# Recurrence: x and z on all four blocks of the array, the identity added in the copy of prod

## The reference, cut to what matters

```
def wkv7_step(S, inp):
    r, w, k, v, a, b = inp
    sa = jnp.einsum('bhvk,bhk->bhv', S, a)
    S = S * w[:, :, None, :] + sa[..., None] * b[:, :, None, :] + v[..., None] * k[:, :, None, :]
    return S, jnp.einsum('bhvk,bhk->bhv', S, r)

for d in range(2):
    S_c, yc_d = direction(cx, d, S0)
    _, yl_d = direction(lat, d, S_c)
```

## Time and profile before

| | us |
|---|---|
| median of 3 runs | 4211.17 (4208.52 to 4217.72) |
| the profiled execution | 4217.04 |
| its span, first to last instruction | 4215.2 |
| mean granted clock of TensorE | 0.940 |

### The profile page before, as it was taken

How to read it: one execution, slowest core, us unless ns; L and a number is a source line. 1 busy time by engine, 2 the same in 40 slices (tenths; PEclk the granted TensorE clock), 3 DMA queues, 4 the chain that set the end, 5 groups by cost and what they waited for, 6 DMA issues and landing times. The chain is left out here.

```text
span 4215.2 us, 70162 instructions
## 1 busy us (share of the span) xinstructions
PE 3678.9 (87%) x29588; PEld 2620.8 (62%) x29588; DVE 2002.5 (48%) x3720; ACT 1101.5 (26%) x2219; POOL 640.1 (15%) x675
## 2 busy tenths in 40 slices
PE   5978869999979897989868777698999997899999
PEld 4844663444458774868753222297778776677877
DVE  3688750000045566757660000155567446656762
ACT  2124510000024313223220000124532223663221
POOL 0014400111113202415200000013200001440000
PEclk8988989999989998989979999999999998899999
DMA  4142258999940321010249999820122231012222
GB/s 169 61 158 61 76 212 329 393 391 391 377 148 36 98 100 53 3 42 3 69 181 394 402 405 403 336 81 21 47 95 95 93 98 42 21 35 73 94 95 80
DMA packets 195487, 659.98 MB, mean 157 GB/s; under 512 B 27708, under 2 KB 86076, under 8 KB 145368
## 3 DMA queue, kind: packets, MB, share of 16 engines
q1 hardware_dynamic: 182392, 621.16, 38.8%
q0 software_dynamic: 12784, 34.35, 3.1%
HBM read 626.01 MB, written 29.44 MB: 155 GB/s over the span
## 5 line engine op out<-in xcount | busy, mean ns | idle before, releaser
L3469 DVE TENSOR_TENSOR ffn_w_lo<-ffn_landing,ffn_w_hi 128x1024 fp32r<-128x1024 f32 x128 | 156.8, 1225 | 295.4 <-ACT ffn_w_hi L3447 295.4
L3418 PE MATMUL ffn_ps<-ffn_inT_hi,ffn_w_hi 128*128 128x512 f32 x704 | 277.8, 395 | 3.5 <-PEq L70 3.5
L3418 PE MATMUL ffn_ps<-ffn_inT_lo,ffn_w_hi 128*128 128x512 f32 x704 | 278.8, 396 | 0.0
L3418 PE MATMUL ffn_ps<-ffn_inT_hi,ffn_w_lo 128*128 128x512 f32 x704 | 277.9, 395 | 0.0
L2044 PE MATMUL up_ps<-w_quarter,rowsT 128*64 128x512 f32 x1024 | 235.9, 602 | 36.7 <-DMA w_quarter<-in_moe_w 36.7
L2044 PE MATMUL down_ps<-w_quarter,hiddenT 128*64 128x512 f32 x1024 | 235.0, 598 | 31.7 <-DMA w_quarter<-in_moe_w 29.7
L2044 PE MATMUL gate_ps<-w_quarter,rowsT 128*64 128x512 f32 x1024 | 235.5, 605 | 29.5 <-DMA w_quarter<-in_moe_w 20.7
L1960 POOL DMA_INDIRECT summed_dram<-gains_then_rows,part_row x48 | 74.7, 1556 | 929.2 <-DVE gains_then_rows L2174 924.3
L2167 DVE TENSOR_TENSOR gain_then_hidden<-up_ps,gain_then_hidden 128x768 f32<-128x768 f32 (+1 forms) x32 | 26.4, 824 | 348.3 <-PE up_ps L2056 179.0
L2044 PEld LDWEIGHTS down_ps<-w_quarter,hiddenT 128*64 128x64 f32 x1024 | 68.5, 136 | 189.3 <-issue 130.1
L2104 ACT ACTIVATE rowsT<-misc_ps 128x384 f32<-128x384 f32 (+1 forms) x64 | 27.8, 437 | 599.0 <-PE misc_ps L2033 597.3
(11 more groups left out here) (722 smaller groups left out, 8416.8 us busy)
## 6 DMA issues: line engine op xcount, KB each, us to landing
w_quarter<-in_moe_w SPq DMA_DIRECT2D x384, 1024.0 KB, 17.8
ffn_landing<-in_f_w_up SPq DMA_DIRECT2D x88, 512.0 KB, 3.5
ada_ring<-in_ada_w SPq DMA_DIRECT2D x80, 512.0 KB, 5.6
ffn_landing<-in_f_w_down SPq DMA_DIRECT2D x44, 512.0 KB, 3.5
w_landing<-in_od_w_in SPq DMA_DIRECT2D x13, 1024.0 KB, 6.3
w_landing<-in_a_w_in SPq DMA_DIRECT2D x12, 1024.0 KB, 5.1
ada_landing<-in_ada_w SPq DMA_DIRECT2D x8, 1024.0 KB, 12.6
w_landing<-in_ev_w_in SPq DMA_DIRECT2D x6, 1024.0 KB, 5.0
```

Of the source, the lines that this page charges most:

```text
L3418: mm = nc.tensor.matmul(ps[c % 4][:, :], w[:, c % NP, cols], h[:, k, :], start=(k + i == 0), stop=(k == KD - 1 and i == 2))
L3469: nc.vector.tensor_tensor(wl[:, c % NP, :], land[:, c % NL, :], wh[:, c % NP, :].bitcast(F32), ALU.subtract).then_inc(split, 1)
```

## The change

x and z are no longer increments. prod's copy adds the identity (VectorE, from PSUM, L2654 of the changed kernel), so that x_ps = (I + prod)' X and z_ps = X' (I + prod) are the new X and Z, which ScalarE copies (L2548, L2550). z is written to the other half of the partitions than x, and so is L_off's gram: prod reads half o and writes half hb, x reads hb and writes hb, z reads hb and writes o. x and z of a head are issued in turn, x, z, x, z, over four different blocks. L is kept with its halves swapped, by a gram of its own (`gram_l`, 24 matmuls into `prod_ps`), while the start of X comes from `x_ps`. At a boundary ScalarE copies the filled-in block (z_full) ahead of L. VectorE does new_state, scaled_state and output_rows after the prod adds of level 0, decay_sums and effective_keys ahead of a masked copy, and scaled_queries after the last level.

```diff
+    other = (half[1], half[0])
@@ scalar
-                for n in range(LV):
-                    rows = slice(0, P) if n < LC else co
+                for n in range(LC - 1):
                     for g in range(2):
-                        act.wait_ge(sm["prod_done"], 2 * LV * s + 2 * n + g + 1)
-                        nc.scalar.activation(Pm[g][rows, :, :], b4(bp[g])[rows], ACT.Copy).then_inc(sm["prod_kept"], 1)
+                        act.wait_ge(sm["xz_done"], 2 * LC * s + 2 * n + g + 1)
+                        nc.scalar.activation(Zb[g][:, :, :], b4(bz[g]), ACT.Copy).then_inc(sm["z_kept"], 1)
+                    for g in range(2):
+                        nc.scalar.activation(X[g][:, :, :], b4(bx[g]), ACT.Copy).then_inc(sm["x_kept"], 1)
@@ vector
                 for n in range(LC):
-                    i = 2 * LC * s + 2 * n
                     for g in range(2):
-                        dve.wait_ge(sm["xz_done"], i + g + 1)
...
-                            tt(Zb[g][:, :, :], Zb[g][:, :, :], b4(bz[g]), ALU.add).then_inc(sm["z_kept"], 1)
-                            tt(X[g][:, :, :], X[g][:, :, :], b4(bx[g]), ALU.add).then_inc(sm["x_kept"], 1)
...
+                        dve.wait_ge(sm["prod_done"], 2 * LV * s + 2 * n + g + 1)
+                        tt(Pm[g][:, :, :], b4(bp[g]), wide(eye), ALU.add).then_inc(sm["prod_kept"], 1)
+                    if n == 0 and s:
+                        if lat[s - 1]:
+                            output_rows(s - 1)
+                        new_state(s - 1)
+                        scaled_state(s)
                     if n == 1:
+                        if ahead:
+                            decay_sums(s + 1)
                         if lat[s]:
                             masked(QB, incl, "gram_q", "qb_kept", 2 * lats[s])
-                        if ahead:
-                            decay_sums(s + 1)
@@ tensor
-                gram_blocks(bx, A, Bt, diagonal + [(ro, co, 4 * B)], "gram_x")
+                gram_blocks(bx, A, Bt, diagonal, "gram_x")
                 if s:
                     between(s - 1)
-                gram_blocks(bz, Bt, A, diagonal, "gram_z")
+                gram_blocks(bp, A, Bt, swapped + [(ro, ro, co, 4 * B)], "gram_l")
+                gram_blocks(bz, Bt, A, swapped, "gram_z")
...
-                            for hb in half if n < LC - 1 else [co]:
-                                mm(bx[g][hb, cols], Pm[g][hb, q, :], X[g][hb, q, :], start=True, stop=True,
-                                   skip_group_check=True)
-                            for hb in half:
-                                ins = mm(bz[g][hb, cols], X[g][hb, q, :], Pm[g][hb, q, :], start=True, stop=True,
+                            for hb, o in zip(half, other):
+                                if n < LC - 1 or hb == co:
+                                    mm(bx[g][hb, cols], Pm[g][hb, q, :], X[g][hb, q, :], start=True, stop=True,
+                                       skip_group_check=True)
+                                ins = mm(bz[g][o, cols], X[g][hb, q, :], Pm[g][hb, q, :], start=True, stop=True,
                                          skip_group_check=True)
```

More of the change, by code:

```diff
@@ L2551, in _ @@
                     if n == 2 and s + 1 < NCHUNK:
-                        exponentials(s + 1)
+                        key_exponentials(s + 1)
+                    if n == 3 and s + 1 < NCHUNK:
+                        query_exponentials(s + 1)
+                for g in range(2):
+                    act.wait_ge(sm["xz_done"], 2 * LC * (s + 1) - 1 + g)
+                    nc.scalar.activation(X[g][co, :, :], b4(bx[g])[co], ACT.Copy)
+                    nc.scalar.activation(Z[s % 2][g][co, :, co], b4(bz[g])[ro], ACT.Copy).then_inc(sm["x_kept"], 1)
+                for g in range(2):
+                    act.wait_ge(sm["prod_done"], 2 * LV * (s + 1) - 1 + g)
+                    nc.scalar.activation(Pm[g][co, :, :], b4(bp[g])[co], ACT.Copy).then_inc(sm["last_kept"], 1)
         @block.vector
@@ L2600, in scaled_state, with state_sum @@
                 ins.then_inc(sm["s0_ready"], 1)
-            def new_state(s):
-                c = order[s] // RC
+            def state_sum(s):
                 dve.wait_ge(sm["state_done"], s + 1)
@@ L2608, in new_state @@
                 ins.then_inc(sm["state_read"], 1)
+            def new_state(s):
+                c = order[s] // RC
                 dve.wait_ge(sm["state_read"], s + 1)
@@ L2634, in _ @@
                 if s:
[L2635 to L2638, removed]
+                    state_sum(s - 1)
                 for n in range(LC):
-                    i = 2 * LC * s + 2 * n
                     for g in range(2):
-                        dve.wait_ge(sm["xz_done"], i + g + 1)
[L2643 to L2647, removed]
-                            tt(Zb[g][:, :, :], Zb[g][:, :, :], b4(bz[g]), ALU.add).then_inc(sm["z_kept"], 1)
-                            tt(X[g][:, :, :], X[g][:, :, :], b4(bx[g]), ALU.add).then_inc(sm["x_kept"], 1)
-                        else:
-                            tt(Z[s % 2][g][ro, :, ro], Zb[g][ro, :, :], b4(bz[g])[ro], ALU.add).then_inc(sm["z_kept"], 1)
+                        dve.wait_ge(sm["prod_done"], 2 * LV * s + 2 * n + g + 1)
+                        tt(Pm[g][:, :, :], b4(bp[g]), wide(eye), ALU.add).then_inc(sm["prod_kept"], 1)
@@ L2657, in _ @@
                     if n == 2:
-                        masked(MT, strict, "gram_m", "mt_kept", 2 * s)
                         if ahead:
                             effective_keys(s + 1)
-                    if n == 3:
-                        if lat[s]:
-                            masked(QK, incl, "gram_k", "qk_kept", 2 * lats[s])
-                        if ahead:
-                            scaled_queries(s + 1)
+                        masked(MT, strict, "gram_m", "mt_kept", 2 * s)
+                    if n == 3 and lat[s]:
+                        masked(QK, incl, "gram_k", "qk_kept", 2 * lats[s])
@@ L2666, in _ @@
                 for g in range(2):
-                    tt(X[g][co, :, :], X[g][co, :, :], b4(bx[g])[co], ALU.add)
-                    tt(Z[s % 2][g][co, :, co], Zb[g][co, :, :], b4(bz[g])[co], ALU.add).then_inc(sm["x_kept"], 1)
+                    dve.wait_ge(sm["xz_done"], 2 * LC * (s + 1) - 1 + g)
+                    nc.vector.tensor_copy(Z[s % 2][g][ro, :, ro], b4(bz[g])[co]).then_inc(sm["ro_kept"], 1)
+                if ahead:
+                    scaled_queries(s + 1)
                 dve.wait_ge(sm["rhs_done"], s + 1)
@@ L2670, in _ @@
                 nc.vector.tensor_copy(rhs[:, :], m[0][:, :]).then_inc(sm["rhs_kept"], 1)
+            state_sum(NCHUNK - 1)
             new_state(NCHUNK - 1)
@@ L2701, in gram_blocks @@
                                 ins.then_inc(sm[sem], 1)
-            diagonal = [(half[0], half[0], 0), (half[1], half[1], 0)]
+            diagonal = [(hb, hb, hb, 0) for hb in half]
+            swapped = [(o, hb, hb, 0) for hb, o in zip(half, other)]
             def solve(s):
@@ L2804, in _ @@
                 for n in range(LC):
-                    i = 2 * LV * s + 2 * n
                     kept = 2 * LC * s + 2 * n
+                    if n == 0:
+                        pe.wait_ge(sm["between_kept"], 2 * s + 2)
                     for g in range(2):
```

61 lines of the change are left out of this document (30 added, 31 removed).

## The result

| | before | changed |
|---|---|---|
| median, us | 4213.31 (4208.52 to 4217.72, 4 runs) | 4183.95 (4180.34 to 4186.46, 4 runs) |
| ratio | | 0.9922, 95% interval 0.9905 to 0.9940 |
| profiled execution, its span | 4217.04, 4215.2 | 4186.46, 4184.3 |
| granted clock, mean | 0.940 | 0.939 |

What follows compares the result with a forecast made beforehand. TensorE's matmul stream, with a short prod-to-x handover, was taken to bound each level; chunk gains and pass start less boundary costs gave 15.1 us a pass, 30 us in two, median 4181 us, range 4162 to 4205.

Steps and rivals of the forecast that it cites:

- x and z on four blocks: Both passes: x and z at 16 ns a record, 1.02 us a level for 1.89; last level 18 ns, 0.86 us.
- The first rival: The four blocks don't overlap: x and z keep 29.6 ns a record, 4227 us; chance 0.07.
- The floor between starts: Blocks overlap, but records start no closer than near 24 ns: 4203 to 4211 us, no change; chance 0.05.
- Handover prod to x: With VectorE adding the identity and no copies ahead, x starts 1.25 us after prod, against 1.17 before.
- The masked copies ahead of the add: On VectorE they hold prod's add: x starts 1.92 us after prod, 0.67 us lost 28 times, 18.8 us.
- the rival without a stall: VectorE doesn't hold the add on prod, the 28 stalls of 0.67 us vanish: 4162 us; chance 0.08.
- Image chunk: First prod to the right-hand side: 18.09 us for 20.62, 2.53 less in each image chunk.
- Context chunk: Each context chunk takes 15.13 us for 18.43, 3.3 less.
- Boundary: 48 more gram records cost 0.86 us behind image chunks, three times a pass; 0.15 gained behind context chunks.
- Start of a pass: inverse_start gets x from PSUM before L's copy; counted as 0.7 us gained a pass, an estimate.
- Handovers that cost more: 0.2 us more at each of 60 levels, twice, up to 24 us: 4205 us; chance 0.10.
- The clock: More waits could bring more stretches at 1.2 GHz in the passes; few expected, no size or separate chance given.

Runs made afterwards that it cites:

- e1: Changed kernel with z, L and Z in the same half as x, so prod, x and z use only the two diagonal blocks: 4231.31 us, ratio 1.0025.
- e3: Changed kernel with one masked copy ahead of the prod adds and one behind, half of effective_keys a level later in image chunks: 4169.25 us, ratio 0.9886.
- e2: Kernel before with x and z on four blocks, the second gram and earlier z_full copy, but without the moved identity: 4174.28 us, ratio 0.9899.
- e5: Changed kernel itself run again, unaltered, on another chip: 4184.59 us over 6 runs, ratio 0.9922.
- e8: Changed kernel with x, x, z, z issued for each pair of halves instead of x, z, x, z: 4172.80 us, a single run.
- e6: e3 without the second gram; ScalarE makes L's swapped copy from x_ps instead: 4161.07 us, ratio 0.9868.
- e7: Changed kernel with all 8 x matmuls of a group issued first, then all 8 z: 4196.13 us, a single run.
- e4: Changed kernel with the 48 records of the gram of L issued twice, same output: 4187.39 us, ratio 0.9931.

## Why the prediction was right, and where it was off

The median came to 4183.95 us for 4181 forecast, and each step can be held against a row.

- **x and z on four blocks: right.** 15.0 ns a record for 16, 0.94 us a level for 1.02. The last level's 48 records over three blocks take 19.9 ns each, for the 18 that I took from gram. The first rival (30 ns, 4227 us) is refuted by the trace, and e1, which makes it come true, has about the price that it gave, 16 us: at the full clock its passes are 15.4 us longer than before, and its median is 13.3 us above that of the kernel before on its chip. The floor between starts is refuted as well. The Trainium skill ("TensorE: Matmul & The Clock Gate", "Wait — 56ns, not 53.3ns?") puts it at about 25 ns, at which the change would have brought nothing; starts 15 ns apart on different blocks disagree.
- **Handover prod to x: right.** x starts 1.21 us after prod at levels 0 and 1, for 1.25.
- **The masked copies ahead of the add: right.** x at 1.84, 1.78 and 1.78 us after prod for 1.92, so 0.57 to 0.63 us is lost each time for 0.67. e3 took the stall away and gained 15 us, which settles it between the forecast and the rival without a stall (4162): the queue was there, and the 18.8 us that both set for it was somewhat high.
- **Image chunk: right, a little too small.** 17.60 us to the right-hand side for 18.09. The difference is in the three terms above, 0.04 to 0.19 us a level.
- **Context chunk: right.** 15.3 us in the first pass and 15.6 in the second for 15.13.
- **Boundary: right.** From the right-hand side to the next prod 0.74 us more behind image chunks in the first pass and 0.88 in the second, for 0.86; behind context chunks nothing (10.64 before, 10.66 after, second pass) for 0.15 gained.
- **Start of a pass: size off.** 6.46 us became 5.16, 1.3 less for 0.7. Chunk 0's first level went from 5.80 us to 3.71 and from 6.20 to 4.50, 3.8 us in all where the sum counts 0.7 a pass: it took all context chunks to be like chunk 1 at the full clock, and 2.6 us of these 3.8 is the clock.
- **Handovers that cost more** (4205): no. The price of the moved identity that e2 shows, 2.5 us, is small. The Trainium skill's warning ("TensorEngine Tiling (Array Packing)", "PSUM Bottleneck") that faster packing may leave the copies as the bound holds here in another form: not the rate of the copies but the place of one in VectorE's queue holds TensorE.
- **The clock: a term that I didn't size.** I had written that few stretches at the lower level were to be expected, and looked only at the levels of an image chunk. The tail was in the earlier trace rows, inside the passes' 0.94 and 0.96, and prod at the start of a pass, 1.97 us for 32 records that take 1.15 elsewhere, in the earlier trace rows; I didn't ask which stretches made the means. As profiled, the clock gave 4.1 us back in the other stretches and took 4.6 with one more tail, so that it all but cancelled. That it did is luck, and no step of the sum foresaw it.
- **The sum.** The passes' own work became 33.7 us shorter by the estimate above, not 30, and 33.2 as profiled; the rest of the program took 2.3 us more, for which the sum has no term. So the 29.4 us by the medians for 30 forecast are partly misses that cancel: the work was underestimated by some 4 us, and the rest of the program took over half of it back.

Open: what decides whether a tail runs at the one level or the other. In e5 the single runs lie 26 us apart, with a mean clock of 0.936 in the longest (4195 us) and 0.944 in the shortest (4169), so the clock goes with the time, but no run here sets it. The changed kernel had both tails partly at the lower level in both of its profiles, e8, with the same levels, in neither: whether chance or the kernel decides is not shown. Open too are the late levels in e3 and e6.

## What to carry to other kernels

Small matmuls that use only the diagonal blocks of the array leave half of it idle: write one of two products to the other half of the partitions, and issue them in turn, not one group after the other. When a stream of matmuls gets shorter, list for each handover what stands ahead of it in the queue of the engine that makes it; here a 1.28 us masked copy ahead of a 0.4 us add cost half as much as the change brought. When a change is worth less than about 10 us in 4200, compare the same stretch at the same granted clock, and look for every stretch at the lower level, not only the longest; here the tails alone gave 37.8 us where all of them gave 33.7.

## What the runs showed of the hardware that I had not expected

- 64x64 float32 records on four different blocks start 15.0 ns apart, on two 30 ns, on three 19.9 ns: that is about one record every 60 ns for each block, whatever the others do (e1, e8, changed kernel; 62 ns in the earlier trace rows, where one block works alone).
- A record overtakes waiting ones if its block is free, but only about six of them (e7): grouped by product 21 to 22 ns, interleaved 15.
- The order x, z, x, z or x, x, z, z makes no difference (e8).
- The same 16 records take 2.00 us at the full clock and 3.68 us in a stretch of the tail at 0.50; the tail of a pass takes 15.2 or 19.8 us.
- Issuing 48 more records costs 0.94 us, 19.6 ns each, at a boundary where TensorE has nothing to wait for (e4).
